# A reordered opening of the gated DeltaNet heads: one Gram product, decays on ScalarE, side work on GpSimd

## The reference, cut to what matters

```
gc = cumsum(g)                              # within a chunk
decay = exp(where(i >= j, gc_i - gc_j, -inf))
kb = k * beta
lmat = where(i > j, (kb @ k.T) * decay, 0)
rhs = [v * beta, kb * exp(gc)]
u, w = triangular_solve(lmat, rhs)          # unit diagonal
k_dec = k * exp(gc_last - gc);  g_last = exp(gc_last)
per chunk:
  v_new = u - w @ s
  o = (q * exp(gc)) @ s + ((q @ k.T) * decay) @ v_new
  s = s * g_last + k_dec.T @ v_new
```

## Time and profile before

| | us |
|---|---|
| median of three runs | 4918.99 |
| lowest, highest | 4915.6, 4931.08 |
| profiled execution, its own time | 4920.18 |
| profiled execution, span | 4918.3 |

### The profile page before, as it was taken

The page is one execution under the profiler, slowest core; times in us unless marked ns, Lnnn a source line. Parts: engine busy times, 40 slices in busy tenths (PEclk is TensorE's granted clock), DMA queues, the critical chain, the costliest instruction groups (busy, mean ns, idle before and its releaser), DMA issues. The chain is left out here.

```text
span 4918.3 us, 52675 instructions
## 1 busy us (share of the span) xinstructions
PE 4060.4 (83%) x19068; PEld 3233.2 (66%) x19068; DVE 3022.4 (61%) x3602; ACT 1895.9 (39%) x2236; POOL 768.2 (16%) x364
## 2 busy tenths in 40 slices
PE   3956799958997999678888888849999597699995
PEld 2723587734734777467777877737888476588884
DVE  6753477344835874355555555538999543699995
ACT  2032332212203332333233323317777422477773
POOL 0200000001200000010000000013555100255551
PEclk9977899969998999778889888869999898799997
DMA  4310155211601452100000000019999510799993
GB/s 175 137 69 19 56 183 180 87 57 65 253 25 34 154 185 82 34 18 18 17 17 17 17 17 34 1 58 391 356 362 372 187 69 19 283 374 359 367 359 118
DMA packets 372150, 691.39 MB, mean 141 GB/s; under 512 B 38327, under 2 KB 118327, under 8 KB 371320
## 3 DMA queue, kind: packets, MB, share of 16 engines
q1 hardware_dynamic: 327696, 639.79, 36.5%
q10 hardware_dynamic: 25032, 32.98, 2.0%
q0 software_dynamic: 19296, 16.94, 1.0%
HBM read 700.01 MB, written 41.00 MB: 151 GB/s over the span
## 5 line engine op out<-in xcount | busy, mean ns | idle before, releaser
L505 PE MATMUL psum<-work_rounded 128*128 128x512 f32 x3504 | 1159.2, 401 | 119.6 <-DVE fixed_rounded L499 59.3
L499 DVE TENSOR_TENSOR ring_rounded<-ring,work_rounded 128x2048 fp32r<-128x2048 f32 (+1 forms) x445 | 816.0, 1836 | 422.9 <-ACT work_rounded L494 292.7
L505 PEld LDWEIGHTS psum<-work_rounded 128*128 128x128 f32 x3504 | 668.1, 192 | 282.5 <-issue 141.8
L505 PE MATMUL psum<-work_rounded,fixed_rounded 128*128 128x512 f32 x2544 | 781.6, 402 | 32.8 <-DVE fixed_rounded L2719 16.7
L505 PE MATMUL psum<-work_rounded,ring_rounded 128*128 128x512 f32 (+1 forms) x1824 | 726.4, 398 | 0.0
L2637 ACT ACTIVATE work_rounded<-ring 128x2048 fp32r<-128x2048 f32 x256 | 491.0, 1920 | 276.1 <-PE psum L505 173.1
L494 ACT ACTIVATE work_rounded<-ring 128x1024 fp32r<-128x1024 f32 x204 | 215.9, 1059 | 976.5 <-PE psum L505 711.6
L505 PEld LDWEIGHTS psum<-work_rounded,fixed_rounded 128*128 128x128 f32 x2544 | 482.6, 190 | 151.4 <-issue 22.2
L505 PE MATMUL psum<-fixed_rounded,work_rounded 128*128 128x512 f32 (+1 forms) x1088 | 431.1, 396 | 0.0
L505 PEld LDWEIGHTS psum<-work_rounded,ring_rounded 128*128 128x128 f32 x1824 | 351.1, 192 | 80.9
L499 DVE TENSOR_TENSOR work_rounded<-work,work_rounded 128x2048 fp32r<-128x2048 f32 (+1 forms) x196 | 337.8, 1733 | 41.5 <-ACT work_rounded L2637 37.6
(11 more groups left out here) (313 smaller groups left out, 6269.2 us busy)
## 6 DMA issues: line engine op xcount, KB each, us to landing
ring<-in_w SPq DMA_DIRECT2D x128, 2048.0 KB, 12.5
work<-in_w SPq DMA_DIRECT2D x64, 2048.0 KB, 12.0
ring<-in_mod_w SPq DMA_DIRECT2D x24, 2048.0 KB, 8.0
ring<-in_ada_w SPq DMA_DIRECT2D x24, 2048.0 KB, 7.9
ring<-in_ffn_w_in SPq DMA_DIRECT2D x44, 1024.0 KB, 7.6
ring<-in_ffn_w_out SPq DMA_DIRECT2D x10, 2048.0 KB, 7.8
ring<-in_w_in_a SPq DMA_DIRECT2D x32, 512.0 KB, 6.1
ring<-in_hy_w_in SPq DMA_DIRECT2D x6, 2048.0 KB, 8.0
```

Source lines behind the costliest of these rows:

```text
L499: return eng.tensor_tensor(c.rounded(v), v, c.rounded(v_high), ALU.subtract)
L505: ins = pe.matmul(out, c.rounded(w), c.rounded(x), start=(start and i == 0), stop=(stop and i == 2))
```

## The change

- TensorE makes lane 0's rows as soon as the columns of g and beta are there, ahead of the transposes of v and k, and lane 1's rows behind them.
- One product of the keys with themselves (six chunks) serves both lanes, and one product of keys with queries too. Before, each lane scaled the keys by beta first and had its own products. Now VectorE multiplies the beta rows in afterwards (`first`).
- ScalarE forms the decay with Relu, with the cumulated gate as the bias, and Exp from the rows (`decay`), where VectorE had subtracted and clipped in six instructions per lane. Exp of the cumulated gates of a column is one small instruction (`eg`), and VectorE makes minus beta times it (`bg`). The last decays (`kd`) are read out of the decay matrix.
- The scan multiplies the unscaled keys (`kz`) with the state, and applies `bg` after the product; beta times v comes ready from GpSimd.
- GpSimd (`pool_head`) takes the copy of z, the triangular mask of the scores, q times the growth, the masks of the inversion's first level, beta times v and the copy of the keys.
- The high parts of the next head's weights are made one by one behind levels 1 to 4 of the inversion.

```diff
@@ -1558,6 +1558,7 @@
 G_MIX = G_LANE + 2 * LANE
+G_EG = G_MIX + KD * T + T + 16
 LEVELS = 7
@@ -1644,8 +1645,8 @@
     PER = {"slab": 64, "full": 6, "centre": 5, "conv": 5, "silu": 5, "square": 3, "sumsq": 4,
-           "std": 2, "root": 2, "unit": 2, "turned": 2, "turned_out": 2, "cols": 2, "rows": 2, "grown": 2, "kb": 2, "darg": 2,
-           "dexp": 2, "kk": 2, "kdarg": 2, "mt": 12, "a": 12, "a_out": 24, "x": 12, "upd": 13,
+           "std": 2, "root": 2, "unit": 2, "turned": 2, "turned_out": 2, "cols": 2, "rows": 2, "grown": 2, "tt": 2, "eg": 1,
+           "flat": 2, "kk": 2, "m1": 2, "side": 1, "mt": 10, "a": 12, "a_out": 24, "x": 12, "upd": 13,
            "z": 12, "r": 12, "vn": 12, "vn_out": 13, "vnd": 12, "su": 12, "s": 13, "o": 1,
@@ -1656,6 +1657,9 @@
         self.g, self.beta, self.gcum, self.kd, self.gl = (v(G_COL + 12 * i, 2, NTA) for i in range(5))
+        self.eg, self.bg = v(G_EG, 2, NTA), v(G_EG + 12, 2, NTA)
+        self.kz = v(G_VT, KEYS)
+        self.settled = core.shared("expert_settled", 0)[0]
         self.order = [[0, 1, 2, 3, 4, 5], [1, 0, 5, 4, 3, 2]]
@@ -1672,10 +1676,9 @@
-    def weights_high(self, act, h):
+    def weight_high(self, act, h, part):
         self.wait(act, h, "slab", 64)
-        for part in range(4):
-            high(self.c, act, self.slab_high[:, part], self.slab_dst()[:, part]).then_inc(self.made, 1)
+        high(self.c, act, self.slab_high[:, part], self.slab_dst()[:, part]).then_inc(self.made, 1)
@@ -1685,7 +1688,54 @@
         with pool.Fori(0, DHEADS - 1) as h:
+            self.pool_head(pool, h)
             self.weights_low(pool, h + 1)
+            self.wait(pool, h, "end", 3)
+        self.pool_head(pool, DHEADS - 1)
+    def pool_head(self, pool, h):
+        s = self.s
+        def scores(l):
+            tri = self.c.const(("cum_f", "cum_b")[l]).unsqueeze(1).to_broadcast([P, NT, P])
+            self.wait(pool, h, "flat", l + 1)
+            pool.tensor_tensor(self.lane(l, L_QK, NT, P), self.lane(l, L_M, NTA, P)[:, NTC:NTA, :], tri, ALU.mult)
+        def grown(l):
+            last = P - 1 if l == 0 else 0
+            g = self.lane(l, L_KBG, KEYS)
+            self.wait(pool, h, "grown", l + 1)
+            pool.tensor_tensor(self.lane(l, L_QD, T), self.q, g[:, TC:KEYS], ALU.mult)
+            pool.tensor_copy(self.gl[:, l, :], g.rearrange("p (t n) -> p t n", n=P)[:, :, last])
+        def mask(l):
+            m = self.c.view(G_MASK + P * (7 * l + 1), P).unsqueeze(1).to_broadcast([P, NTA, P])
+            self.wait(pool, h, "tt", l + 1)
+            pool.sem_inc(self.settled, 1)
+            pool.drain()
+            pool.tensor_tensor(self.lane(l, L_M, NTA, P), self.lane(l, L_L, NTA, P), m, ALU.mult).then_inc(s["m1"], 1)
+        self.wait(pool, h, "silu", 5)
+        pool.sem_inc(self.settled, 1)
+        pool.tensor_copy(self.z_now, self.z)
+        scores(0)
+        grown(0)
+        mask(0)
+        scores(1)
+        mask(1)
+        grown(1)
+        self.wait(pool, h, "turned_out", 2)
+        pool.sem_inc(self.settled, 1)
+        pool.drain()
+        for l in range(2):
+            beta = self.beta[:, l, :].unsqueeze(2).to_broadcast([P, NTA, P])
+            pool.tensor_tensor(self.lane(l, L_KBG, NTA, P), self.vt, beta, ALU.mult)
+        pool.drain()
+        pool.tensor_copy(self.kz, self.k)
+        pool.drain().then_inc(s["side"], 1)
@@ -1755,7 +1805,8 @@
     def scalar(self, act):
-        self.weights_high(act, 0)
+        for part in range(4):
+            self.weight_high(act, 0, part)
         for x_high, x, _ in self.src.values():
@@ -1861,6 +1912,17 @@
+        def rows(l):
+            for t in range(NTA):
+                pe.matmul(c.pair(4 * l, KEYS)[:, P * t:P * t + P], self.g[:, l, t:t + 1].to_broadcast([P, P]),
+                          c.const(("cum_f", "cum_b")[l]), start=True, stop=True)
+                ins = pe.matmul(c.pair(4 * l + 2, KEYS)[:, P * t:P * t + P],
+                                self.beta[:, l, t:t + 1].to_broadcast([P, P]), ident, start=True, stop=True)
+            ins.then_inc(s["rows"], 1)
+        self.wait_mixed(pe, h, "cols", 1)
+        rows(0)
         self.wait(pe, h, "unit", 2)
@@ -1868,32 +1930,23 @@
         ins.then_inc(s["turned"], 1)
-        self.wait_mixed(pe, h, "cols", 1)
         self.wait(pe, h, "turned_out", 2)
-        for l in range(2):
...
-            self.wait(pe, h, "mt", l + 1)
+        rows(1)
+        self.wait(pe, h, "grown", 1)
+        for t in range(NTA):
+            cols = slice(P * t, P * t + P)
+            ins = pe.matmul(c.pair(0, KEYS)[:, cols], self.k[:, cols], self.k[:, cols], start=True, stop=True)
+        ins.then_inc(s["kk"], 1)
+        self.wait(pe, h, "grown", 2)
+        for t in range(NTC, NTA):
+            ins = pe.matmul(c.ps[:, 4, P * (t - NTC):P * (t - NTC) + P], self.k[:, P * t:P * t + P],
+                            self.q[:, P * (t - NTC):P * (t - NTC) + P], start=True, stop=True)
+        ins.then_inc(s["kk"], 1)
+        def place(l):
+            self.wait(pe, h, "tt", l + 1)
             for t in range(NTA):
@@ -1902,7 +1955,11 @@
                 T_, M = self.lane(l, L_T, NTA, P), self.lane(l, L_M, NTA, P)
-                self.wait(pe, h, "mt", i + 1)
+                if v == 1:
+                    place(l)
+                    self.wait(pe, h, "m1", l + 1)
+                else:
+                    self.wait(pe, h, "mt", i - 1)
                 self.wait(pe, h, "upd", i + 1)
@@ -1926,9 +1983,10 @@
                     self.wait(pe, h, "upd", 13)
+                    self.wait(pe, h, "side", 1)
                 else:
                     self.wait(pe, h, "s", i - 1)
-                pe.matmul(c.ps[:, 2 * l, 0:P], self.lane(l, L_KBG, NTA, P)[:, t, :], self.st(l, 0), start=True, stop=True)\
+                pe.matmul(c.ps[:, 2 * l, 0:P], self.kz[:, P * t:P * t + P], self.st(l, 0), start=True, stop=True)\
                     .then_inc(s["z"], 1)
@@ -1980,21 +2038,29 @@
         c, s = self.c, self.s
+        self.wait_mixed(act, h, "cols", 1)
+        act.activation(self.eg, self.gcum, ACT.Exp).then_inc(s["eg"], 1)
+        def decay(l):
+            m, rows = self.lane(l, L_M, NTA, P), c.pair(4 * l, KEYS).rearrange("p (t n) -> p t n", n=P)
+            self.wait(act, h, "rows", l + 1)
+            for t in range(NTA):
+                act.activation(m[:, t, :], rows[:, t, :], ACT.Relu, scale=-1.0, bias=self.gcum[:, l, t:t + 1])
+            act.drain()
+            flat = self.lane(l, L_M, KEYS)
+            act.activation(flat, flat, ACT.Exp, scale=-1.0).then_inc(s["flat"], 1)
+        def grow(l):
+            act.activation(self.lane(l, L_KBG, KEYS), c.pair(4 * l, KEYS), ACT.Exp).then_inc(s["grown"], 1)
+        decay(0)
         self.wait(act, h, "turned", 2)
         act.activation(self.kt.rearrange("p t n -> p (t n)"), c.pair(6, KEYS), ACT.Copy).then_inc(s["turned_out"], 1)
-        for l in range(2):
...
-            self.weights_high(act, h + 1)
+        grow(0)
+        decay(1)
+        grow(1)
         for v in range(1, LEVELS):
@@ -2005,6 +2071,8 @@
                 act.activation(self.lane(l, L_TT, KEYS), c.pair(4 * l + 2, KEYS), ACT.Copy).then_inc(s["a_out"], 1)
+            if more and v <= 4:
+                self.weight_high(act, h + 1, v - 1)
         for i in range(2 * NTA):
@@ -2032,61 +2100,54 @@
         dve.drain().then_inc(s["cols"], 1)
-        self.wait(dve, h, "silu", 5)
-        dve.tensor_copy(self.z_now, self.z)
         self.wait(dve, h, "turned", 1)
         dve.tensor_copy(self.vt.rearrange("p t n -> p (t n)"), c.pair(4, KEYS)).then_inc(s["turned_out"], 1)
+        self.wait(dve, h, "eg", 1)
+        dve.scalar_tensor_tensor(out=self.bg, in0=self.eg, scalar=-1.0, in1=self.beta, op0=ALU.mult, op1=ALU.mult)
+        ident = c.const("ident").unsqueeze(1).to_broadcast([P, NTA, P])
+        def mask(v, l, out):
+            m = c.view(G_MASK + P * (7 * l + v), P).unsqueeze(1).to_broadcast([P, NTA, P])
+            return dve.tensor_tensor(self.lane(l, out, NTA, P), self.lane(l, L_L, NTA, P), m, ALU.mult)
+        def decayed(l):
+            last = P - 1 if l == 0 else 0
+            self.wait(dve, h, "flat", l + 1)
+            dve.tensor_copy(self.kd[:, l, :], self.lane(l, L_M, NTA, P)[:, :, last])
+            self.wait(dve, h, "kk", 1)
+            dve.tensor_tensor(self.lane(l, L_L, KEYS), self.lane(l, L_M, KEYS), c.pair(0, KEYS), ALU.mult)
+            dve.drain()
+        def first(l):
+            v, TT = self.lane(l, L_L, KEYS), self.lane(l, L_TT, NTA, P)
+            dve.tensor_tensor(v, v, c.pair(4 * l + 2, KEYS), ALU.mult)
+            dve.drain()
+            mask(0, l, L_TT)
+            dve.drain()
+            dve.tensor_tensor(TT, TT, ident, ALU.add)
+            dve.drain().then_inc(s["tt"], 1)
+        decayed(0)
+        first(0)
+        dve.transpose(self.lane(0, L_T, KEYS), self.lane(0, L_TT, KEYS))
+        decayed(1)
+        dve.drain().then_inc(s["upd"], 1)
+        first(1)
```

(58 more changed lines are left out.)

## The result

The changed kernel takes 4855.38 us against 4920.4 (medians of four runs each): a ratio of 0.9865, 95% interval 0.9848 to 0.9882. That is 65 us less where I had forecast 39, inside the range (4853 to 4904) by 2 us.

What follows compares the result with a forecast made beforehand. The opening was taken as bound by handovers through VectorE, inversion and scan by TensorE. Opening -77.4, high parts +26.6 and level 1 side work +12 gave -38.8 us from 4918.99: 4880 us, range 4853 to 4904.

Steps and rivals of the forecast that it cites:

- The stretched products: Opening: four VectorE operations take longer while GpSimd makes the low weight parts, 7.6 us per looped head.
- The new opening: Head start to first update product: 30.1 us at the low clock, from 40.7 in looped heads; 77.4 us saved in all.
- The row that I leaned on: Clock evidence: TensorE busy 7.95 of 17 us from 2434.5 at granted clock 0.50, after waiting 8.6 us for VectorE.
- GpSimd's prices: Opening: 768-column two-input products on GpSimd take 1.6 us, scaled from a 1024-column row at 2.12 us.
- The high parts in the inversion: Inversion levels 1 to 4: each part between ScalarE's copies costs 0.95 us, 26.6 us over seven heads.
- The first rival: Inversion: the weight parts are hidden there and cost nothing, 27 us more gain, 4853 us; chance 0.14.
- The low parts: Inversion: GpSimd's low parts (2.1 us) start after VectorE's mask of lane 1 has begun; costed at nothing.
- The third rival: Inversion: GpSimd's low parts also stop VectorE's transposes and PSUM readers, 20 us slower, 4939 us; chance 0.06.
- Level 1: Inversion's first level: GpSimd's beta times v meets VectorE's two masks, 1.5 us in eight heads, 12 us.
- The tail: End of each looped head, from the last keys-with-state product to the next head's copies: taken as unchanged, 0 us.
- The scan costs the same: Scan: its VectorE operation keeps one PSUM and one SBUF operand and the SyncE loads stay, so no change.
- the 126 to 127 that I gave as a sign: Whole looped head: length would be about 126 to 127 us in place of 131.6.

Runs made afterwards that it cites:

- b_gap: Kernel before the change, only the next head's high weight parts moved from the opening into ScalarE's idle time in inversion levels 1 to 4; 4855.0 us.
- turns_first: Changed kernel with the transposes of v and k first again and lane 0's rows behind them; 4850.8 us, one run.
- the kernel with all three edits: Changed kernel with high parts in ScalarE's idle time, GpSimd's side work behind the low parts, and transposes first; 4822.7 us, ratio 0.9796.
- low_late: Changed kernel with each of GpSimd's low weight parts held until both update products of the next level are through; 4856.8 us, one run.
- w_gap: Changed kernel with each high part moved ahead, between ScalarE's copies of the two products and of the two inverses; 4846.1 us, ratio 0.9846.
- gap_side: w_gap with GpSimd's side work for the scan moved behind the four low weight parts in the seven looped heads; 4842.5 us, ratio 0.9834.

## Why the prediction was right, and where it missed

- *The stretched products.* Right: 7.6 us per looped head were worked out, b_gap took 7.9 out of head 3 and 54.3 out of the seven by that one cause.
- *The new opening.* Right in its steps up to the last product (27.3 us against 27.5), 1.2 us too long at its end. I took the low clock from the last masks on. After the change the low stretch, apart from one in the head's first 4.4 us, was 2414.3 to 2421.2 only, and the last product ran at the high clock: 1.44 us where I had 2.6. The row that I leaned on fits less well than I said: the clock was low from 2434.5 on, but TensorE's wait of 8.6 us ran from 2430.0 to 2438.6, so half of it lay inside that stretch. The low price does occur: turns_first and the kernel with all three edits paid 2.5 to 2.7 us for that product in eleven of their sixteen heads.
- *GpSimd's prices.* 1.81 us for 768 columns and 1.26 for 512 where I had 1.6 and 1.06 from the 1024-column row. That row is of another stage; the low parts of these heads, as wide, take 2.35 us each where VectorE is out of the way. The estimate of 1.7 from the page "GPSIMD Engine Reference" of the Trainium skill ("Performance versus the Vector engine") was nearer. On the path this counts once per head.
- *The high parts in the inversion.* Right for levels 2 to 4: 0.95 taken, 0.94 shown by low_late. The first rival (hidden) falls where the parts were put, and holds about 4 us earlier in the level, as w_gap shows.
- *The low parts.* The statement that VectorE's mask has begun first was right in two looped heads by 0.17 us and wrong in five by 0.3 us. The cost was small, 0.28 a level, because the transposes behind it had slack. With it levels 2 to 4 cost 4.1 us more than forecast. The third rival's premise, a hold on PSUM readers too, falls: transposes keep 0.98 us beside the low part.
- *Level 1.* I charged it 0.95 for the part and 1.5 for GpSimd's side work, 7.9 us in all. It took 7.09, or 7.6 to 7.7 in heads 1 and 5, whose clock was low there. The side work is 1.06 of the 1.63 excess (gap_side against w_gap), and the high part with its low part 0.57 (the changed kernel against w_gap). Over all heads this is 4.8 us less than forecast, which covers the 4.1 of the levels behind it. That the term as a whole came within 0.7 us is luck.
- *The tail.* The step that failed: "The scan costs the same", with everything behind it taken as unchanged. The scan did, 34.07 us against 33.97 in a looped head; the tail lost 2.4 us a head by the clock. This is 16.7 of the 25.7 us that were missed by the spans, the opening 8.3 and the inversion 0.7. For this reason and the opening's, a head took 122.8 us and not the 126 to 127 that I gave as a sign.

## What to carry to other kernels

Look at what moves a neighbour before what shortens a chain: here one work package that triggered another engine's burst was worth the whole of a large rewrite, whose own 30 us came out only when its costs in the inversion were moved away (4822.7 us against b_gap's 4855.0). When work is moved into a busy stage, put it where its engine waits in each period, and see what its consumer then lies beside. And price code that an edit does not touch at two clock levels: its clock can change with the timing ahead of it. When a sum comes out right, check its terms too: here two of them were off by 4 to 5 us each way.

## What the runs showed of the hardware

A VectorE copy of 128x6 float32 elements from SBUF to SBUF took 1.09 us where it began during GpSimd's product, and ended with it; else it took 0.17. One input is enough to be held. The Trainium skill's page "SBUF — State Buffer" ("SBUF: two separate sides") counts VectorE's two-port modes among the holders of the shared pair, which agrees if this copy ran in one. The transposes of 768 columns out of PSUM kept 0.98 us beside GpSimd (w_gap).

The same 99 or so TensorE instructions of a tail took 22.2 us at a granted clock of 0.92 and 25.9 at 0.69, in neighbouring heads (low_late).
